# Three bodies behind a branch: the order of expert widths in a two-layer hybrid backbone

## The chip, the core and the metric

The kernel runs on one core of a Trainium2 chip. The metric is the device time of one execution in microseconds (us). TensorE (PE, its sequencer PEq or PEldq), VectorE (DVE), ScalarE (ACT), GpSimd (POOL) and SyncE (SP) each run a stream of instructions of their own and meet through semaphores. All DMAs of weights are issued by SP.

## What is computed

Two layers over 256 latent tokens and 256 context tokens, model width 1024. Both layers mix tokens (gated linear attention and a short convolution). The first layer's channel mixer is a dense SwiGLU, the second's is a mixture of experts over the 256 latent tokens only:

```
def swiglu(h, w1, w3, w2):
    return (jax.nn.silu(h @ w1) * (h @ w3)) @ w2

logits = (h @ w_r).astype(jnp.float32)
vals, idx = lax.top_k(logits, TOP_K)                  # TOP_K = 2 of N_EXPERTS = 8
wts = jax.nn.softmax(vals, axis=-1)
comb = jnp.sum(jax.nn.one_hot(idx, N_EXPERTS) * wts[..., None], axis=-2)
for e in range(N_EXPERTS):
    out = out + comb[..., e:e + 1] * swiglu(h, w1e[e], w3e[e], w2e[e])
```

An expert's three matrices are 1024 x 3584, 1024 x 3584 and 3584 x 1024 in float32. How many tokens choose an expert is known only when the kernel runs: 512 choices over 8 experts, 64 on average.

## The kernel before

Everything up to the router runs without branches. Then each expert `e` is worked through in turn. SP issues its weights without a branch: 42 pieces of 1 MB per expert (`ORDER`, L74), into a ring of 10 slots (`ESLOTS`), 6 pieces for each of the 7 blocks (`NB`) of 512 hidden columns: four of the gate and up matrices (L535), two of the down matrix (L539). A piece may be loaded when the piece ten places ahead of it in the ring's order has been used; `frees` (L478) on PE says so.

PE, ACT and DVE each hold three bodies for each expert, and pick one by its number of tokens:

- `few(e)`: up to 64 tokens (`FEW`). PE multiplies in float32, 64 columns wide (L947 gate and up, L973 down). ACT applies Silu, DVE the product.
- `mid(e)`: 65 to 128 tokens. Each weight piece is split into a rounded part (ACT, L1428) and a remainder (DVE, `low_part`, L1520), and PE makes three products (L1017, L1019, L1024).
- `big(e)`: 129 to 256 tokens, two tiles of float32 products.

The bodies end alike: PE gathers the tokens of expert `e + 1` (L902), turns its weights (L909) and, in `add_slots`, spreads the expert's output over the tokens (L927). DVE adds these sums to the accumulator (L1950). PE may begin `e + 1` only when all four sums are added (`sum_done`), and a middle body also needs its first rounded part from ACT.

The choice is made anew on each of the three engines. Each reads the count of expert `e` from `cnt_i` into a register (L1157 PE, L1471 ACT, L2061 DVE) and calls `by_width`, which writes two nested tests. In the instruction stream the bodies stand one after another: test, `few`, an unconditional jump to the next expert, second test, `mid`, a jump, `big`, a jump. A test that fails jumps to what stands behind the body. The counts are made by PE (L889, L890) and copied to `cnt_i` by DVE (L1906) before `route_ready` lets the experts start.

In the streams of PE the three bodies hold 831, 1186 and 1681 instructions (1 for a wait or branch, 2 for a rounded matmul or a transpose, 4 for a float32 matmul). On ACT they hold about 35, 117 and 46.

With this kernel's inputs experts 0, 1 and 4 take `mid` and the five others `few`.

## Time and profile before

| | before |
|---|---|
| median of 3 runs | 2024.03 us (2020.35 to 2026.72) |
| profiled execution | 2023.0 us |
| its span | 2021.2 us |
| mean granted clock of PE in it | 0.94 of full speed |
| PE busy | 1799.6 us (89%) |
| DVE, ACT busy | 819.5 us (41%), 524.7 us (26%) |
| the experts | from 1038 to about 2000 us of the span |

The times below are of one profiled execution, in us from the span's start, and durations of single instructions in ns. A row of the timeline gives start, duration, engine, line, operation, what it writes and reads, how many, and in brackets how long its engine was idle before it and what ended that; "issue" means that nothing which the profile shows was waited for. Branches, register loads and waits belong to the sequencers (PEldq, ACTq, DVEq) and are not counted as busy; the view of a source line shows them with their durations.

### The profile page before, as it was taken

The page shows a single profiled execution, that of the slowest core. Times are in us where ns is not written, and L with a number is a line of the kernel's source. Part 1 is how long each engine was busy: PE and PEld are TensorE (multiplying, and loading weights), DVE is VectorE, ACT ScalarE, POOL GpSimd, SP SyncE. Part 2 cuts the span into 40 slices and gives each one's busy share as a digit, 9 for nine tenths or more (in the row PEclk, how much of TensorE's full clock was granted, in tenths as well). Part 3 has the DMA queues.
Part 4 walks back from the last instruction along what each step waited for, and adds up shares of the span by engine and source line. Part 5 has one row for each costly group of instructions (what it writes and reads, how often), then busy time and mean ns, then how long its engine had stood idle before and what let it go on. Part 6 is the DMA issues. An engine that isn't in the chain of part 4 may idle for free.

```text
span 2021.2 us, 19505 instructions
## 1 busy us (share of the span) xinstructions
PE 1799.6 (89%) x7958; PEld 1117.3 (55%) x7958; DVE 819.5 (41%) x1146; ACT 524.7 (26%) x656; POOL 2.3 (0%) x12
## 2 busy tenths in 40 slices
PE   5999979999999998997979989898877998887876
PEld 2344435378887875476778768633325883332322
DVE  1044341354443766135269788601105871010102
ACT  3321023330000013212357567400004750000001
POOL 0000000000000000000000000000000000000000
PEclk9899999999999998898879999999998999889998
DMA  9323198523322023222339979799999998999994
GB/s 342 122 83 125 35 365 308 159 91 112 97 84 97 18 76 125 83 84 84 115 137 376 344 263 376 265 359 394 393 396 353 374 346 301 396 391 395 394 394 172
DMA packets 223828, 476.21 MB, mean 236 GB/s; under 512 B 9906, under 2 KB 32724, under 8 KB 223700
## 3 DMA queue, kind: packets, MB, share of 16 engines
q1 hardware_dynamic: 222176, 474.24, 64.0%
q8 instruction: 86, 1.41, 0.3%
q10 hardware_dynamic: 1524, 0.21, 0.1%
q14 instruction: 42, 0.34, 0.0%
HBM read 473.38 MB, written 1.05 MB: 235 GB/s over the span
## 4 chain that ended last, share of the span: by engine, by line
PE 72%; SPq 12%; DMA 7%; issue 3%; DVE 3%; ACT 2%; ACTq 0%; DVEq 0%; POOL 0%; POOLq 0%
PE ps L646 9%; SPq L535 9%; PE ps L652 6%; PE ps L654 6%; PE ps L653 6%; PE ps L1017 6%; PE ps L1019 6%; PE ps L947 6%; PE ps L1024 6%; PE ps L813 4%; DMA ring<-in_e_w 4%; SPq L539 3%; PE ps L704 3%; PE ps L688 3%; PE ps L591 2%
## 5 line engine op out<-in xcount | busy, mean ns | idle before, releaser
L947 PE MATMUL ps<-ring,work 128*64 128x512 f32 x1120 | 286.3, 661 | 85.9 <-DMA ring<-in_e_w 64.4
L947 PEld LDWEIGHTS ps<-ring,work 128*64 128x64 f32 x1120 | 91.6, 151 | 256.7 <-issue 256.7
L1520 DVE TENSOR_TENSOR ring_rounded<-ring,hT_rounded 128x2048 fp32r<-128x2048 f32 x84 | 191.7, 2289 | 28.1 <-ACT hT_rounded L1428 21.7
L1967 DVE TENSOR_TENSOR mixT<-work,ps 64x256 f32<-64x256 f32 x70 | 29.7, 424 | 425.4 <-ACT work L1409 424.3
L646 PE MATMUL ps<-hT,ring 128*128 128x512 f32 (+2 forms) x544 | 182.4, 494 | 0.0
L1428 ACT CAST hT_rounded<-ring 128x2048 fp32r<-128x2048 f32 x84 | 159.9, 1911 | 44.8 <-PE ps L1019 35.0
L646 PEld LDWEIGHTS ps<-hT,ring 128*128 128x128 f32 (+1 forms) x544 | 99.6, 185 | 80.2 <-issue 73.0
L652 PE MATMUL ps<-mixT_rounded,work_rounded 128*128 128x512 f32 x352 | 138.4, 393 | 6.0 <-DVE hT_rounded L1520 5.2
L653 PE MATMUL ps<-hT_rounded,work_rounded 128*128 128x512 f32 x352 | 138.1, 392 | 0.0
L654 PE MATMUL ps<-mixT_rounded,ring_rounded 128*128 128x512 f32 x352 | 137.9, 392 | 0.0
L973 PE MATMUL ps<-ring,mixT 128*64 128x512 f32 x560 | 125.7, 593 | 0.0
L1017 PE MATMUL ps<-hT_rounded,work_rounded 128*128 128x512 f32 x252 | 102.7, 407 | 22.9 <-issue 19.6
L1520 DVE TENSOR_TENSOR ring_rounded<-ring,norms_rounded 128x2048 fp32r<-128x2048 f32 x42 | 96.1, 2289 | 22.8 <-ACT norms_rounded L1428 22.8
L1019 PE MATMUL ps<-hT_rounded,work_rounded 128*128 128x512 f32 x252 | 100.7, 400 | 0.0
L1517 DVE CAST work_rounded<-ring 128x1024 fp32r<-128x1024 f32 (+1 forms) x88 | 49.1, 558 | 123.8 <-PE ps L654 123.8
L1024 PE MATMUL ps<-ring_rounded,work_rounded 128*128 128x512 f32 x336 | 91.4, 394 | 0.0
L1520 DVE TENSOR_TENSOR ring_rounded<-ring,work_rounded 128x1024 fp32r<-128x1024 f32 (+1 forms) x88 | 84.1, 955 | 1.5
L813 PE MATMUL ps<-mixT,ring 128*128 128x512 f32 (+1 forms) x256 | 83.1, 486 | 1.3 <-issue 1.3
L1411 ACT COPY mixT<-ps 128x256 f32<-128x256 f32 x35 | 13.0, 372 | 272.2 <-PE ps L961 272.2
L973 PEld LDWEIGHTS ps<-ring,mixT 128*64 128x64 f32 x560 | 41.0, 137 | 76.7 <-issue 70.2
L1428 ACT CAST norms_rounded<-ring 128x2048 fp32r<-128x2048 f32 x42 | 80.3, 1912 | 9.3 <-issue 6.9
L652 PEld LDWEIGHTS ps<-mixT_rounded,work_rounded 128*128 128x128 f32 x352 | 66.8, 190 | 21.1 <-issue 7.2
(228 smaller groups left out, 2400.1 us busy)
## 6 DMA issues: line engine op xcount, KB each, us to landing
ring<-in_e_w SPq DMA_DIRECT2D x336, 1024.0 KB, 13.7
ring<-in_w_mod SPq DMA_DIRECT2D x24, 2048.0 KB, 16.9
ring<-in_w_in SPq DMA_DIRECT2D x12, 2048.0 KB, 11.1
ring<-in_w SPq DMA_DIRECT2D x22, 1024.0 KB, 7.9
ring<-in_w_out SPq DMA_DIRECT2D x4, 2048.0 KB, 14.1
ring<-in_w SPq DMA_DIRECT2D x4, 2048.0 KB, 7.8
ring<-in_w SPq DMA_DIRECT2D x2, 1536.0 KB, 6.6
mixT<-in_ctx SPq DMA_DIRECT2D x2, 512.0 KB, 4.2
```

The lines of the kernel that those rows point to most:

```text
L535: sp.dma_start(dst.rearrange("p (k n) -> p k n", k=4), rows(w[0, e, k0 * P:(k0 + 4) * P], b * BLK, BLK)).then_inc(piece_in[s], 16)
L646: ins = pe.matmul(acc[0:width, 0:TOK - c0], w[:, k, m * P:m * P + width], hT[:, k, c0:], start=(k == 0), stop=(k == KD - 1))
L652: pe.matmul(acc, w_high_, x_high_, start=first, stop=False)
L653: pe.matmul(acc, w_high_, x_low_, start=False, stop=False)
L654: return pe.matmul(acc, w_low_, x_high_, start=False, stop=last)
L947: ins = pe.matmul(acc[H * w:H * w + H, :], x[:, k, 0:H], piece_words(e, b, 2 * half + w)[:, kk * BLK:(kk + 1) * BLK], start=(k == 0), stop ...
L973: ins = pe.matmul(ps[0][H * half:H * half + H, :], eh[:, b % 2, ((j % 2) * 2 + j // 2) * H:][:, 0:H], piece_words(e, b, 4 + i)[:, o:o + BL ...
L1017: pe.matmul(outs[q], high[q], w_high_[:, cols], start=q < first, stop=False, skip_group_check=True)
L1019: ins = pe.matmul(outs[q], low[q], w_high_[:, cols], start=False, stop=False, skip_group_check=True)
L1024: ins = pe.matmul(outs[q], high[q], w_low_[:, q * BLK:(q + 1) * BLK], start=False, stop=q >= 4 - last, skip_group_check=True)
L1428: act.copy(highs[at_ % HIGHS], piece_words(e, b, i)).then_inc(high_ready, 1)
L1520: return dve.tensor_tensor(dst, src, high, ALU.subtract)
```

## The change

DVE turns the counts into a class before the experts start: 0 for 65 to 128 tokens (`MID`), 1 for more (`BIG`), 2 for up to 64 (`SMALL`). The three engines load the class in place of the count, and `by_width` tests it so that the body for 65 to 128 tokens stands first in each stream, that for more second and the narrow one last. The bodies themselves are the same. The new lines stand some lines further down: L85 becomes L89, L88 L92, L947 L951, L1017 L1021.

```
-def by_width(eng, chosen, few, mid, big):
-
-    with eng.If(chosen < FEW + 1):
-        few()
+
+MID, BIG, SMALL = 0, 1, 2
+
+
+def by_width(eng, width, few, mid, big):
+
+    with eng.If(width < MID + 1):
+        mid()
     with eng.Else():
-        with eng.If(chosen < P + 1):
-            mid()
+        with eng.If(width < BIG + 1):
+            big()
         with eng.Else():
-            big()
+            few()
...
-                chosen = pe.value_load(cnt_i[0:1, e:e + 1], min_val=0, max_val=SEQ)
-                by_width(pe, chosen, lambda: few(e), lambda: mid(e), lambda: big(e))
+                width = pe.value_load(width_i[0:1, e:e + 1], min_val=0, max_val=SMALL)
+                by_width(pe, width, lambda: few(e), lambda: mid(e), lambda: big(e))
...
-            drains(dve.tensor_copy(cnt_i[:], acc[0:1, 2 * NE:3 * NE]), ("pos",))
+            width, chosen = small[0:1, 15, :], acc[0:1, 2 * NE:3 * NE]
+            step(dve.tensor_scalar(width, chosen, FEW + 0.5, float(SMALL), ALU.is_lt, ALU.mult))
             wait_step()
+            drains(dve.scalar_tensor_tensor(out=width, in0=chosen, scalar=P + 0.5, in1=width,
+                                            op0=ALU.is_gt, op1=ALU.add), ("pos",))
             step(dve.tensor_scalar(place, place, 1.0, None, ALU.subtract))
             step(dve.memset(yacc, 0.0))
 
             step(dve.memset(hid, 0.0))
             wait_step()
             wait_drained(dve, ("pos",))
+            step(dve.tensor_copy(width_i[:], width))
+            wait_step()
             dve.tensor_copy(small[:, 14, 2:3], ones[:, 0:1]).then_inc(route_ready, 1)
```

The same two lines change on ACT and on DVE as on PE.

In PE's stream, where the bodies of expert 0 end and those of expert 1 begin, stood before:

```order
L902 MATMUL ps<-work 128x128 x16
L909 MATMUL ps<-ident,work 128x128 x2
L927 MATMUL ps<-work 128x256 x16
L90 UNCONDITIONAL_BRANCH
L1157 TENSOR_LOAD cnt_i
L1157 ISA x2
L85 COMPARE_AND_BRANCH
L947 MATMUL ps<-ring,work 64x512 x24
```

and stands now:

```order
L906 MATMUL ps<-work 128x128 x8
L913 MATMUL ps<-ident,work 128x128 x2
L931 MATMUL ps<-work 128x256 x8
L94 UNCONDITIONAL_BRANCH
L1161 TENSOR_LOAD width_i
L1161 ISA x2
L89 COMPARE_AND_BRANCH
L1021 MATMUL ps<-hT_rounded,work_rounded 128x512
```

The last body of an expert was the wide one (L927 sixteen times) and is the narrow one, and behind the next expert's test stands the middle body (L1021) in place of the narrow one (L947).

In PE's stream, where the first body of expert 0 ends, stood before the end of the narrow body, the jump and the second test, then the middle body:

```order
L961 MATMUL ps<-ident,mixT 128x128 x2
L973 MATMUL ps<-ring,mixT 64x512 x16
L902 MATMUL ps<-work 128x128 x8
L909 MATMUL ps<-ident,work 128x128 x2
L927 MATMUL ps<-work 128x256 x8
L85 UNCONDITIONAL_BRANCH
L88 COMPARE_AND_BRANCH
```

Now the end of the middle body stands there, then the second test and the wide body:

```order
L1023 MATMUL ps<-norms_rounded,mixT_rounded 128x512
L1028 MATMUL ps<-ring_rounded,mixT_rounded 128x512 x4
L906 MATMUL ps<-work 128x128 x8
L913 MATMUL ps<-ident,work 128x128 x2
L931 MATMUL ps<-work 128x256 x8
L89 UNCONDITIONAL_BRANCH
L92 COMPARE_AND_BRANCH
```

In DVE's stream, between the counts and the first selection of tokens, stood before:

```order
L1904 SCALAR_TENSOR_TENSOR small<-ps,small 128x16
L1906 CAST cnt_i<-ps 1x8
L1908 TENSOR_SCALAR small<-small 128x16
L1909 MEMSET work 128x2048
L1911 MEMSET mixT 128x1024
L1914 COPY small<-ones 128x1
L1923 TENSOR_SCALAR work<-work,small 128x256
```

and stands now:

```order
L1908 SCALAR_TENSOR_TENSOR small<-ps,small 128x16
L1911 TENSOR_SCALAR small<-ps 1x8
L1913 SCALAR_TENSOR_TENSOR small<-ps,small 1x8
L1915 TENSOR_SCALAR small<-small 128x16
L1916 MEMSET work 128x2048
L1918 MEMSET mixT 128x1024
L1921 CAST width_i<-small 1x8
L1923 COPY small<-ones 128x1
L1932 TENSOR_SCALAR work<-work,small 128x256
```

The copy of the counts has become two small operations, and a third one writes the classes as integers ahead of the operation that lets the other engines go (L1923).

## Rows read from the trace of the kernel before

**Rows 1.** Timeline of PE: first matmul of experts 0 to 5, first behind the experts.

```profile
1038.06 0.47 PE L1017 MATMUL ps<-hT_rounded,work_rounded 128*128 128x512 f32 x1 [3.25 <-ACT hT_rounded L1428]
...
1175.06 0.77 PE L1017 MATMUL ps<-hT_rounded,work_rounded 128*128 128x512 f32 x1 [7.63 <-issue]
...
1310.39 1.12 PE L947 MATMUL ps<-ring,work 128*64 128x512 f32 x2 [5.72 <-issue]
...
1421.45 1.12 PE L947 MATMUL ps<-ring,work 128*64 128x512 f32 x2 [3.48 <-issue]
...
1539.96 0.76 PE L1017 MATMUL ps<-hT_rounded,work_rounded 128*128 128x512 f32 x1 [11.99 <-issue]
...
1673.31 0.65 PE L947 MATMUL ps<-ring,work 128*64 128x512 f32 x2 [3.58 <-issue]
...
2001.91 0.77 PE L591 MATMUL ps<-norms,ones 128*128 128x256 f32 x1 [2.82 <-ACT norms L1203]
```

**Rows 2.** Lines L85, L88, by stretch: count, ns min/median/max, first to last start.

```profile
L85 PEldq COMPARE_BRANCH  x1: 3865/3865/3865, 1033.5 to 1033.5; - x1
...
L88 PEldq COMPARE_BRANCH  x1: 3270/3270/3270, 1166.3 to 1166.3; - x1
...
L85 PEldq COMPARE_BRANCH  x1: 4122/4122/4122, 1170.3 to 1170.3; - x1
...
L88 PEldq COMPARE_BRANCH  x1: 3702/3702/3702, 1303.5 to 1303.5; - x1
...
L85 PEldq COMPARE_BRANCH  x1: 88/88/88, 1308.0 to 1308.0; - x1
...
L85 PEldq COMPARE_BRANCH  x2: 77/3127/6177, 1413.8 to 1420.7; - x2
...
L85 PEldq COMPARE_BRANCH  x2: 6266/6610/6954, 1525.5 to 1532.5; - x2
...
L88 PEldq COMPARE_BRANCH  x1: 3340/3340/3340, 1668.6 to 1668.6; - x1
...
L85 PEldq COMPARE_BRANCH  x2: 77/3186/6296, 1775.7 to 1782.7; - x2
...
L85 PEldq COMPARE_BRANCH  x2: 77/3150/6222, 1887.5 to 1894.4; - x2
...
L85 PEldq COMPARE_BRANCH  x1: 4944/4944/4944, 1996.3 to 1996.3; - x1
```

**Rows 3.** Stretches: length, busy time by engine, PE clock, DMA share, GB/s.

```profile
1305.00:1308.00 3.00, 0.00 (x0) 0.00 (x0) 1.15 (x3) 0.00 (x0) 0.00 (x0) 1.00 0.03 8
1419.00:1422.00 3.00, 0.55 (x2) 0.32 (x4) 0.29 (x1) 0.00 (x0) 0.00 (x0) 0.50 1.06 388
```

**Rows 4.** Page: the instruction queue; the narrow body's first products, five experts.

```profile
q8 instruction: 86, 1.41, 0.3%
...
L947 PE MATMUL ps<-ring,work 128*64 128x512 f32 x1120 | 286.3, 661 | 85.9 <-DMA ring<-in_e_w 64.4
```

**Rows 5.** Issue to landing, L535: all issues, then those at 1426.8, 1788.6, 1900.8.

```profile
DMA to landing us min/median/max: 5.0/12.4/20.2
...
DMA to landing us min/median/max: 8.1/8.1/8.1
...
DMA to landing us min/median/max: 8.3/8.3/8.3
...
DMA to landing us min/median/max: 9.4/9.4/9.4
```

**Rows 6.** Timeline of DVE and ACT: end of expert 3, and the copied counts.

```profile
1527.03 1.88 DVE L1950 TENSOR_TENSOR work<-work,ps 128x512 f32<-128x512 f32 x3 [0.17 <-PE ps L927]
...
1527.36 1.90 ACT L1428 CAST hT_rounded<-ring 128x2048 fp32r<-128x2048 f32 x1 [4.53 <-issue]
...
1024.41 0.14 DVE L1906 CAST cnt_i<-ps 1x8 int32<-1x8 f32 x1
```

More of the change, by code:

```diff
@@ L254, in hybrid_backbone @@
         small = sb("small", [P, 16, NE])
-        cnt_i = sb("cnt_i", [1, NE], I32)
+        width_i = sb("width_i", [1, NE], I32)
         eps = sb("eps", [P, 1])
@@ L1470, in _ @@
             for e in range(NE):
-                chosen = act.value_load(cnt_i[0:1, e:e + 1], min_val=0, max_val=SEQ)
-                by_width(act, chosen, lambda: few(e), lambda: mid(e), lambda: big(e))
+                width = act.value_load(width_i[0:1, e:e + 1], min_val=0, max_val=SMALL)
+                by_width(act, width, lambda: few(e), lambda: mid(e), lambda: big(e))
             act.wait_ge(sum_done, 4 * NE)
@@ L2060, in _ @@
             for e in range(NE):
-                chosen = dve.value_load(cnt_i[0:1, e:e + 1], min_val=0, max_val=SEQ)
-                by_width(dve, chosen, lambda: few(e), lambda: mid(e), lambda: big(e))
+                width = dve.value_load(width_i[0:1, e:e + 1], min_val=0, max_val=SMALL)
+                by_width(dve, width, lambda: few(e), lambda: mid(e), lambda: big(e))
             add_experts(modv[:, 1, 5])
```

## The prediction

> **What bounds the kernel now.** I read first when TensorE starts each expert, then the branches themselves, then the DMA queue. PE's first matmul of each expert stands in [rows 1]: experts 0, 1 and 4 run the body for 65 to 128 tokens (their first matmul is L1017), experts 2, 3, 5, 6 and 7 the narrow one (L947). In every row but the first and the last, what the profile puts before the start is "issue", idle time of 3.5 to 12 us in which the engine waited for nothing that another engine does. [Rows 2] say what it was: the branch instructions on PE's sequencer. A branch that is not taken costs 77 to 88 ns. Every taken one, of either kind, costs microseconds: 3.27, 3.70 and 3.34 (end of the middle body), 3.87 and 4.12 (the jump past the narrow body) where the weight transfers stand still, 6.18, 6.27, 6.30 and 6.22 (end of the narrow body) and 6.95 (the jump past it, before expert 4) where they run, and 4.94 at the very end. [Rows 3] show the two conditions: from 1305 us the ring of weight pieces is full and DMA moves 8 GB/s, from 1419 us it moves 388. The instructions themselves come by DMA, in packets of 1.41 MB / 86 = 16.4 KB ([rows 4]), so a target far away must first be brought in, behind the weights.
>
> What a PE delay costs depends on the body. In the middle body PE is the bound: expert 4 takes 1673.31 - 1539.96 = 133.4 us with its pause ([rows 1]), 3.2 us for each of its 42 pieces of 1.05 MB, and DMA at 388 GB/s needs 2.7. So a delay before experts 0, 1 and 4 counts in full. The narrow body is bound by DMA, and there the issue of the eleventh piece decides, since it waits for the first piece that PE frees. An issue needs at least 5.0 us to land. At experts 3, 6 and 7 that piece landed 8.1, 8.3 and 9.4 us after its issue ([rows 5]): it stood behind others, and could have been issued 3.1, 3.3 and 4.4 us later at no cost. At experts 2 and 5, which follow a middle body, the queue is dry ([rows 3]) and there is no such reserve: PE's delay is the queue's delay, and every later piece inherits it.
>
> **The change part by part.** PE, ACT and DVE get the same new order. I count PE's taken branches between two experts:
> - middle to middle: two before, one now
> - narrow to middle: two before, none now (the narrow body stands last and runs into the next expert's load)
> - middle to narrow: one before, three now (past two bodies; past the middle one; past the one for over 128)
> - narrow to narrow: one before, two now.
>
> *Saved.* Before expert 1 the jump of 4.12 us falls away; PE needs then what follows a branch, about 0.6 us: 4.2 us gained. Before expert 4 both jumps go, 6.27 and 6.95 us, but PE may not start before DVE has added expert 3's sums, which ends at 1527.03 + 1.88 = 1528.9 ([rows 6]). ACT's first cast, now at 1527.36 behind 4.53 us of issue, moves ahead of that with its own jumps. So PE starts near 1529.1 in place of 1539.96: 10.9 us gained. Expert 4 then runs with a ring that is less full, but DMA's advantage over the expert, 42 x (3.2 - 2.7) = 21 us, refills it before expert 5 takes its eleventh piece. Together -15.1 us.
>
> *Added, middle to narrow.* The test of the class follows the end of a jump by 0.7 us (1525.5 + 6.27 = 1531.8, then 1532.5). So before expert 5 it came at 1668.6 + 3.34 + 0.7 = 1672.7, and PE started 0.6 us later, at 1673.31. Now that test is a jump, in the same place as the one of 4.12 us, and a second one right behind it. No row shows two with nothing between. Its bounds are the cheapest single jump, 3.3 us, and the one of 4.94 us; I take 4.1, the row where a jump followed a landing most closely without traffic. 4.1 + 4.1 - 0.1 = 8.1 us, all on the path. Before expert 2 the same, less 1.7: there the test ended at 1308.1 and PE began only at 1310.39, 2.3 us later in place of 0.6, and I take this for a packet end close behind the landing (7 instructions, below), which the new landing does not have: 6.4 us. Together 14.5.
>
> *Added, narrow to narrow.* The first jump, with traffic, replaces the one that went (6.2 us either way); the second is new: between 6.2 and 7.8 (6.95 plus the 0.8 by which 4.94 exceeds 4.12), taken at 6.95. PE starts 6.9 us later at experts 3, 6 and 7. Less the reserves 3.1 and 3.3: 3.8 and 3.6 us lost. Expert 7 has one thing more. Counted in the built program (a float32 matmul as two loads and two matmuls) the bodies have 831, 1186 and 1681 instructions. If a packet holds 256 of them, the stop of 1.7 us before expert 2 puts a packet's end 7 instructions behind that landing, at 16068 of PE's stream; 83 packets on, at 37316, lies another, and the changed kernel lands for expert 7's narrow body at 37312, 4 instructions before it. The next packet then has to be waited for: 0 to 6.2 us, a whole fetch in traffic. I take 5.2, since the fetch may be ordered at the landing and about 1 us passes before the fifth instruction. The other landings have 88 instructions or more ahead. So 6.9 + 5.2 - 4.4 = 7.7 us. Together 15.1.
>
> *Nothing or nearly.* DVE's routing gains two operations of about 0.15 us (as L1906, [rows 6]) and one wait on the path ahead of the first gather: +0.4. Before expert 0 PE's jump of 3.87 us goes, but its first matmul waited for ACT's cast ([rows 1]), where only the short jump of ACT goes: -0.4. The jumps that ACT and DVE gain before narrow bodies (4.5 us each by [rows 6], two or three in a row) are covered by PE's own jumps and its first block of matmuls, 286.3 / 35 = 8.2 us ([rows 4]), which both wait for; without that cover the last 4.5 us would stand on the path. At the end PE's 4.94 us go too, but L591 waits for ACT's squares ([rows 1]): 0.
>
> **Sum:** -15.1 + 14.5 + 15.1 + 0 = +14.5 us. On the profiled execution, 2023.0 us (1.8 beyond its span of 2021.2), that is 2037.5. The median of the runs shown lies 1.0 above it; I add half: 2038.
>
> **A rule against the rows.** The untaken branches cost 77 to 88 ns and the taken ones 3.27 us and more ([rows 2]). The Trainium skill ("Advanced Engine Details and Errata", Control Flow Timing) gives about 51 ns for a branch that is always taken and about 108 ns for compare-and-branch. By this the order of the bodies would be worth nothing that can be measured; it fits the untaken branches and not the taken ones.
>
> **The rivals.**
> - *Faster: the second of two adjacent jumps is nearly free.* If the sequencer resolves the second branch before it orders the first target's packet, a pair costs what one costs. For it: ACT and DVE get over short distances without a stop. Against it: the pair before expert 4 cost 6.27 and 6.95, not less. It gives -15.1 + 2.3 + 4.0 + 0 + 0 + 0.8 = -8, so 2015. It decides where a second jump costs below about 2.2 us without and 3.2 us with traffic: there the sum crosses zero. The Trainium skill ("Runtime: NRT & Kernel Launch", Instruction fetch mechanics) gives TensorE an instruction memory of 2048 instructions; by this, targets past 1186 or 1681 could be held already. The jump of 6.95 us went past 831, which speaks against it.
> - *Mild: each second jump at its lower bound, no packet end at expert 7.* 3.3 and 6.2 us: -15.1 + 12.9 + 3.1 + 2.9 + 1.8 = +5.6, so 2029.
> - *Harsh: upper bounds.* 4.9 and 7.8 us: -15.1 + 16.1 + 4.7 + 4.5 + 8.6 = +19; and TensorE, at 0.50 of its clock in the window from 1419 us ([rows 3]), may begin narrow bodies slow for longer: up to 2047.
> - *No effect.* The durations in [rows 2] would be a wait for something that meets PE wherever two bodies meet, whatever stands between, and with branches of 0.1 us the sum is the +0.4 of the routing: 2023.4. Against it: one price with traffic, another without, and none where a branch is not taken.
>
> **How the numbers follow.** Forecast 0.60 (2032 to 2042), harsh 0.12, mild 0.14, no effect 0.05, second jump free 0.09. About 0.3%, 6 us, is what a measurement of this kernel can tell from no change. Faster 0.09; same 0.14 + 0.05 = 0.19; slower 0.72. The range takes in the forecast, the mild case and the harsh one, 2026 to 2047, and leaves out the other two.
>
> **What would show it.** In the changed profile, branch rows on PE: pairs of 4 and 4 us before experts 2 and 5, of 6 and 7 before 3, 6 and 7, and under 0.1 us before 1 and 4. PE's start of expert 4 within 1.5 us of DVE's last L1950. The eleventh piece of experts 3, 6 and 7 landing near 5 us after its issue, since the queue has run dry. Five microseconds between the last branch and the first matmul of expert 7. I am wrong if pairs cost as much as one jump, if the reserve of [rows 5] is larger than landing times tell, or if expert 4 starves because its ring starts less full.

## The result, and the profile after

| | before | after |
|---|---|---|
| median | 2023.85 us (2020.35 to 2026.72) | 2051.95 us (2046.72 to 2052.58) |
| ratio of the runs | | 1.0137, 95% interval 1.0125 to 1.0149 |
| span of the profiled execution | 2021.2 us | 2050.8 us |
| mean granted clock of PE | 0.941 | 0.928 |

The kernel became slower by 28.1 us, where 14 were foretold: the sign was right and the size was half. The measured time lies above the range.

The timeline of PE in the changed kernel shows the first matmul of each expert, the second group of expert 7, and the first matmul behind the experts (start, duration, line, and in brackets the idle time ahead and what ended it). It answers to [rows 1].

```profile
1041.86 0.76 PE L1021 MATMUL ps<-hT_rounded,work_rounded 128*128 128x512 f32 x1 [2.89 <-ACT hT_rounded L1432]
...
1174.90 0.76 PE L1021 MATMUL ps<-hT_rounded,work_rounded 128*128 128x512 f32 x1 [3.89 <-issue]
...
1317.32 1.12 PE L951 MATMUL ps<-ring,work 128*64 128x512 f32 x2 [13.21 <-issue]
...
1435.34 1.12 PE L951 MATMUL ps<-ring,work 128*64 128x512 f32 x2 [10.63 <-issue]
...
1545.16 0.77 PE L1021 MATMUL ps<-hT_rounded,work_rounded 128*128 128x512 f32 x1 [0.98 <-DVE work L1959]
...
1687.63 1.12 PE L951 MATMUL ps<-ring,work 128*64 128x512 f32 x2 [12.39 <-issue]
...
1806.82 1.12 PE L951 MATMUL ps<-ring,work 128*64 128x512 f32 x2 [10.98 <-issue]
...
1925.71 1.94 PE L951 MATMUL ps<-ring,work 128*64 128x512 f32 x2 [11.57 <-issue]
...
1928.72 1.12 PE L951 MATMUL ps<-ring,work 128*64 128x512 f32 x2 [1.07 <-issue]
...
2031.41 1.19 PE L595 MATMUL ps<-norms,ones 128*128 128x256 f32 x2 [2.82 <-ACT norms L1207]
```

Set against the starts before (1038.06, 1175.06, 1310.39, 1421.45, 1539.96, 1673.31, 1783.37, 1895.11, 2001.91), each start less the one before it gives what every expert gained or lost:

| from | to | change, us | PE's jumps there |
|---|---|---|---|
| start | expert 0's first matmul | +3.8 | one fewer |
| 0 | 1 | -4.0 | one fewer |
| 1 | 2 | +7.1 | two more |
| 2 | 3 | +7.0 | one more |
| 3 | 4 | -8.7 | two fewer |
| 4 | 5 | +9.1 | two more |
| 5 | 6 | +9.1 | one more |
| 6 | 7 | +7.2 | one more |
| 7 | end | -1.1 | one fewer |

Of the first 3.8 us, 2.4 stood there before the router's counts were made: the profiled execution after is simply later by that much in a part that the change doesn't touch. Another 0.3 is DVE's new work ahead of the first gather. Most of the rest is the gather itself, 32 products that both kernels have, before and after:

```profile
1029.41 5.17 PE L902 MATMUL ps<-work 128*128 128x128 f32 x32 [5.13 <-DVE work L1925]
```

```profile
1032.10 6.66 PE L906 MATMUL ps<-work 128*128 128x128 f32 x32 [5.44 <-DVE work L1934]
```

Before, the granted clock was 0.50 from 1025.4 to 1032.3 us, after from 1027.8 to 1038.1: the whole gather ran at the lower level (1.2 GHz).

The branches on PE's sequencer, by line and stretch (count, ns, start), answer to [rows 2]:

```profile
L89 PEldq COMPARE_BRANCH  x1: 4344/4344/4344, 1307.3 to 1307.3; - x1
L92 PEldq COMPARE_BRANCH  x1: 5022/5022/5022, 1311.7 to 1311.7; - x1
...
L89 PEldq COMPARE_BRANCH  x1: 6306/6306/6306, 1420.8 to 1420.8; - x1
L92 PEldq COMPARE_BRANCH  x1: 7534/7534/7534, 1427.2 to 1427.2; - x1
...
L89 PEldq COMPARE_BRANCH  x1: 82/82/82, 1540.3 to 1540.3; - x1
...
L89 PEldq COMPARE_BRANCH  x1: 4142/4142/4142, 1678.1 to 1678.1; - x1
L92 PEldq COMPARE_BRANCH  x1: 4719/4719/4719, 1682.3 to 1682.3; - x1
...
L92 PEldq COMPARE_BRANCH  x1: 7562/7562/7562, 1917.6 to 1917.6; - x1
```

The pairs stand where they were foretold. The first of a pair costs about what the single jump in its place cost, 4.1 to 4.3 us without traffic and 6.2 to 6.3 with it. The second, right behind it, costs 4.7 to 5.0 and 7.5 to 7.6: dearer than the values taken (4.1 and 6.95), inside the bounds.

Now the weight queue. The eleventh piece of expert 3 is issued at 1441.7 us, and the view of its line (L539 now, L535 before) gives:

```profile
L539 SPq DMA_DIRECT2D ring<-in_e_w x1: 368/368/368, 1441.7 to 1441.7; - x1
...
DMA to landing us min/median/max: 5.2/5.2/5.2
```

In [rows 5] it took 8.1: the queue has run dry, as foretold, at experts 6 and 7 too (5.2 us each). The windows of expert 3's start show more than that. First before, then after (length, busy time of PE, PEld, DVE, ACT, POOL, granted clock of PE, DMA share, GB/s):

```profile
1413.00:1423.00 10.00, 6.14 (x20) 3.97 (x22) 3.70 (x7) 0.00 (x0) 0.00 (x0) 0.58 1.05 386
1423.00:1433.00 10.00, 10.00 (x44) 3.45 (x42) 0.85 (x2) 0.59 (x1) 0.00 (x0) 0.91 1.04 397
```

```profile
1412.00:1420.00 8.00, 4.94 (x31) 2.90 (x28) 2.32 (x4) 1.65 (x3) 0.00 (x0) 1.00 1.05 384
1420.00:1440.00 20.00, 9.37 (x28) 5.04 (x28) 3.03 (x6) 0.00 (x0) 0.00 (x0) 0.51 0.89 331
1440.00:1448.00 8.00, 8.00 (x38) 2.72 (x34) 0.85 (x2) 0.59 (x1) 0.00 (x0) 0.95 0.63 206
```

Before, PE is at the lower level for about 10 us around the jump. After, it stays there for 20: the second jump's idle 7.5 us, and then the first products. These products free the first piece, so the eleventh piece is issued 6.4 us after PE's start instead of 5.3.

### The profile page after: what moved, and what is told of

The parts are those of the page before. It is cut to its first block, busy times and chain, and to the rows that moved or that the text cites. A ratio compares the mean times of both kernels' runs of the same rounds, so it can differ in the third digit from the quotient of the medians.

```text
span 2050.8 us, 19498 instructions
## 1 busy us (share of the span) xinstructions
PE 1812.9 (88%) x7958; PEld 1123.4 (55%) x7958; DVE 819.9 (40%) x1148; ACT 524.6 (26%) x656; POOL 2.3 (0%) x12
## 3 DMA queue, kind: packets, MB, share of 16 engines
HBM read 473.38 MB, written 1.05 MB: 231 GB/s over the span
## 4 chain that ended last, share of the span: by engine, by line
PE 73%; SPq 11%; DMA 6%; issue 4%; DVE 3%; ACT 2%; ACTq 0%; DVEq 0%; POOL 0%; POOLq 0%
PE ps L650 9%; SPq L539 8%; PE ps L656 6%; PE ps L658 6%; PE ps L951 6%; PE ps L657 6%; PE ps L1021 6%; PE ps L1023 6%; PE ps L1028 5%; PE ps L817 4%; DMA ring<-in_e_w 4%; PE ps L708 3%; SPq L543 3%; PE ps L692 3%; PE ps L595 3%
## 5 line engine op out<-in xcount | busy, mean ns | idle before, releaser
L951 PE MATMUL ps<-ring,work 128*64 128x512 f32 x1120 | 292.0, 669 | 117.4 <-issue 59.9
L951 PEld LDWEIGHTS ps<-ring,work 128*64 128x64 f32 x1120 | 93.4, 153 | 291.7 <-issue 291.7
L1524 DVE TENSOR_TENSOR ring_rounded<-ring,hT_rounded 128x2048 fp32r<-128x2048 f32 x84 | 191.7, 2289 | 13.2 <-ACT hT_rounded L1432 11.8
L1021 PE MATMUL ps<-hT_rounded,work_rounded 128*128 128x512 f32 x252 | 103.1, 409 | 7.8 <-issue 3.9
L1413 ACT ACTIVATE work<-ps 64x512 f32<-64x512 f32 x35 | 20.6, 589 | 244.7 <-PE ps L951 244.7
## 6 DMA issues: line engine op xcount, KB each, us to landing
ring<-in_w_out SPq DMA_DIRECT2D x4, 2048.0 KB, 13.9
```

Source lines behind the costliest of these rows:

```text
L951: ins = pe.matmul(acc[H * w:H * w + H, :], x[:, k, 0:H], piece_words(e, b, 2 * half + w)[:, kk * BLK:(kk + 1) * BLK], start=(k == 0), stop ...
L1021: pe.matmul(outs[q], high[q], w_high_[:, cols], start=q < first, stop=False, skip_group_check=True)
L1524: return dve.tensor_tensor(dst, src, high, ALU.subtract)
```

## The ledger

From the traces of both kernels, for the three narrow-to-narrow places, in us: the later start of PE (beyond the shift of the last piece of the expert before), the longer first block up to the issue of the eleventh piece, the part that the piece's wait in the queue absorbed, and what was lost further on until the expert's last piece.

| expert | PE starts later by | first block | absorbed | further on | sum | forecast |
|---|---|---|---|---|---|---|
| 3 | 7.4 | +1.1 | -2.9 | +2.0 | +7.6 | 6.9 - 3.1 = 3.8 |
| 6 | 7.8 | +1.4 | -3.1 | +1.3 | +7.5 | 6.9 - 3.3 = 3.6 |
| 7 | 7.5 | +1.9 | -4.2 | +1.3 | +6.5 | 6.9 + 5.2 - 4.4 = 7.7 |

The column of sums is the shift of the expert's last piece. The stop of 1.07 us stands in the first block of expert 7. For delays of this size the reserve was read rightly (2.9, 3.1, 4.2 against 3.1, 3.3, 4.4). What was missing are a slower first block and a loss after the queue starts again: within eight pieces behind the dry stretch one piece lands about 1.2 us late, in this kernel and, at experts 2 and 5, in the kernel before as well.

The traces say which piece that is. At expert 6 the 18th piece landed 3.86 us after the 17th, where the others follow each other by 2.6 to 2.7, and the windows from 1831.9 to 1834.6 and from 1834.6 to 1838.5 us, the transfers of the 17th and the 18th, hold:

```profile
q1 hardware_dynamic: 528, 1.05, 105.6%
```

```profile
q1 hardware_dynamic: 747, 1.50, 103.2%
q8 instruction: 1, 0.02, 1.8%
```

One packet of PE's instructions (queue 8) began in the second. The sixteen traces here hold 80 narrow bodies. In 54 the queue was dry, or within 2 us of it, when the eleventh piece was issued, and each has a late piece: in 47 the one during whose transfer PE's first packet of instructions begins, between the 13th and the 26th, in 5 the eleventh itself, again with such a packet, and in 2 the one next to it. In the 26 others PE's packets make no piece late. (At expert 3 after, two are late, the 12th by 1.1 us and the 26th by 0.5.) No experiment was made for this, so the link is read from the traces alone, and why a packet costs something only then is open.

## Experiments

The ratios are to the kernel before on the same chip, with 95% intervals.

### One part of the change alone

PE with the new order, ACT and DVE with the narrow body first (`few_first`):

```
+def few_first(eng, width, few, mid, big):
+    with eng.If(width > BIG):
+        few()
+    with eng.Else():
+        with eng.If(width < MID + 1):
+            mid()
+        with eng.Else():
+            big()
...
-                by_width(act, width, lambda: few(e), lambda: mid(e), lambda: big(e))
+                few_first(act, width, lambda: few(e), lambda: mid(e), lambda: big(e))
...
-                by_width(dve, width, lambda: few(e), lambda: mid(e), lambda: big(e))
+                few_first(dve, width, lambda: few(e), lambda: mid(e), lambda: big(e))
```

> PE alone has the new order of bodies; ACT and DVE keep the narrow body first. Theory A (PE's taken branches are what costs, ACT's and DVE's are covered): as the changed kernel, +25 to +30 us on before, with pairs of 4.3 and 5 us before experts 2 and 5 and of 6.3 and 7.5 before 3, 6 and 7. Before expert 4 ACT's first cast keeps its 4.5 us of issue and DVE its 5.1, so PE may wait for the first remainder: up to 3 us more. Rival B (ACT or DVE carry a good part, since every block passes through them): +15 us or less.

Measured 2056.31 us, 1.0174 (1.0157 to 1.0191), 34 us and so above the 25 to 30 expected. PE's order alone does the harm, and a little more: expert 4, which takes 5.9 us longer than in the changed kernel, now waits for DVE once its own jumps are gone. PE's timeline at expert 4's first product with a remainder:

```profile
1549.40 0.79 PE L1039 MATMUL ps<-ring_rounded,work_rounded 128*128 128x512 f32 x1 [3.67 <-DVE ring_rounded L1535]
```

The other way round, `few_first` on PE and the new order on ACT and DVE:

```
-                by_width(pe, width, lambda: few(e), lambda: mid(e), lambda: big(e))
+                few_first(pe, width, lambda: few(e), lambda: mid(e), lambda: big(e))
```

> ACT and DVE have the new order, PE keeps the narrow body first. Theory A: 0 to +1 us on before, since PE's own jumps are as before and only the routing of the classes is added. Rival B: +10 us or more.

Measured 2026.26 us, 1.0012 (1.0000 to 1.0025): their jumps are covered by PE's, as the prediction had it.

The classes alone, with `few_first` on all three engines:

> Only the classes worked out by DVE, with the old order on all three engines. Theory A: +0.3 to +1 us on before. Rival C (the computing and loading of a class is what costs, the order little): +15 us or more.

Measured 2024.13 us, 1.0011 (1.0002 to 1.0021), 0.4 to 4 us by the interval: the classes themselves are cheap.

### Where the gains and the losses are

The classes, with the middle body first for experts 1 and 4 only (`mid_first`: middle, then narrow, then wide) and `few_first` for the others:

```
-                by_width(pe, width, lambda: few(e), lambda: mid(e), lambda: big(e))
+                (mid_first if e in (1, 4) else few_first)(pe, width, lambda: few(e), lambda: mid(e), lambda: big(e))
```

and so on ACT and DVE.

> Classes as in the change, narrow body first for all experts but 1 and 4, where the middle body stands first and the wide one last. So a jump falls away before experts 1 and 4 and none is added anywhere. Theory A, from the rows: 4.1 us gained before expert 1, 6.9 before expert 4 (its start near 1533 in place of 1540), 0.5 lost for the classes: -10.5 us, between -8 and -12. Rival C: slower by what the classes cost. Rival D (expert 4's lead is eaten by its emptier ring): -5 or less.

Measured 2014.59 us, 0.9956 (0.9939 to 0.9974): expert 1 started 2.9 us earlier and expert 4 another 5.9, less than the 4.1 and 6.9 expected; up to 0.7 us was added at each of the others. The jumps themselves gave back all that was expected (4.1 and 7.1 us from the first jump to the first product). What is missing stands ahead of them, where the clock was low. Expert 0 took 129.5 us up to its jump in place of 128.2, with a granted clock of 0.50 for 6.8 us around its start in place of 3.4. Expert 3's last sums, 2.96 us long before (shown further below), took 4.44:

```profile
1524.18 4.44 PE L953 MATMUL ps<-work 64*128 64x256 f32 x16 [3.06 <-DVE work L2005]
```

The change holds a gain, once it is confined to the experts that take this body.

The kernel before with the narrow body last and reached by one jump in place of two, without classes (the middle and the wide body stand within the outer test):

```
-    with eng.If(chosen < FEW + 1):
-        few()
-    with eng.Else():
+    with eng.If(chosen > FEW):
...
+    with eng.Else():
+        few()
```

> No classes; the counts are tested as before, but the outer test asks for more than 64 tokens and holds the middle and the wide body, and the narrow body is its other branch, last in the stream. A narrow body then costs one jump past both others instead of two, the middle one none. Taken jumps on PE: middle to middle 1, narrow to middle 0, middle to narrow 2, narrow to narrow 1 (before: 2, 2, 1, 1). Theory A (each taken jump on PE has its price, the second of a pair the highest): about 4.2 us gained before expert 1, 8.9 before expert 4; 4.3 added before experts 2 and 5 each, less the 1.7 us stop before expert 2; nothing before 3, 6 and 7, where a jump in replaces a jump out: -6 us, between -9 and -3. Rival E (what costs is that the narrow body stands last, far from the load, not the number of jumps): slower than before by 10 us or more.

Measured 2019.63 us, 0.9983 (0.9974 to 0.9992). Experts 1 and 4 began 3.5 and 9.2 us earlier, 2 and 5, with one jump more than before, 2.1 and 5.5 later. Narrow to narrow has one jump as before, and experts 3, 6 and 7 changed by -0.7, +0.3 and -0.1 us. So it is the number of jumps that counts, not the order of the bodies. The gain stayed at the small end of the range, since 1.9 us were lost behind the start of expert 7, where PE stopped after two products:

```profile
1889.81 1.94 PE L947 MATMUL ps<-ring,work 128*64 128x512 f32 x2 [3.18 <-issue]
1895.22 1.12 PE L947 MATMUL ps<-ring,work 128*64 128x512 f32 x2 [3.47 <-issue]
```

The next packet of instructions began at 1892.7 us, 3.5 after the landing, with weights moving. This is a stop of the kind that the prediction had expected at expert 7 of the changed kernel.

### A second jump right behind a first

The changed kernel with 24 idle instructions (3.6 us) between the two tests on PE:

```
     with eng.Else():
+        if between is not None:
+            for _ in range(24):
+                eng.sem_inc(between, 1)
         with eng.If(width < BIG + 1):
```

> The changed kernel with 24 idle sequencer instructions (3.6 us) on PE between the first and the second test. Theory G (the second jump costs 5.0 and 7.5 us because it is ordered right behind a landing, together with the packet that follows the landing): the second jump falls to 3.3 to 4.3 us before experts 2 and 5, and to 6.2 to 7.0 before 3, 6 and 7. Rival H (its price comes from what it jumps over or from its place): it stays at 4.7 to 5.0 and 7.5. The kernel as a whole is slower than the changed one by 8 to 16 us either way.

Measured 2059.33 us, 1.0178 (1.0159 to 1.0198). Those are 8 us more than the changed kernel, by the ratios. The second jumps, five of them, by line:

```profile
L95 PEldq COMPARE_BRANCH  x5: 3757/6057/6277, 1312.7 to 1927.0; - x5
```

They fell to 3.8 and 3.9 us without traffic and 6.1 to 6.3 with it, from 4.7 to 5.0 and 7.5 to 7.6. The instruction queue shows what adjacency changes. In the changed kernel, the second jump before expert 7 runs from 1917.6 us, and the windows 1914.9 to 1916.1 (the first jump's fetch) and 1920.8 to 1921.6 (the second's) hold, in packets, MB and share:

```profile
q8 instruction: 1, 0.02, 5.5%
...
q8 instruction: 2, 0.03, 28.1%
```

For one jump one packet comes. For the second, two come together. I read them as the one that follows the first landing in the stream, which no jump asked for, and the target; the record of a packet does not say which it is. In the spaced kernel each second jump has one packet of its own again. No packet of PE's queue (q8) moves between 1917.6 and 1920.8. In the trace of the packets, the two took 1.37 and 2.22 us, one alone about 1.05. The packet after a jump starts 3.7 us after the jump where weights are moving and about 1 us after it where they are not. The difference of 2.7 us is as long as one weight piece takes at 388 GB/s; that the packet stands behind just one piece is a reading, not shown.

### What a delay of PE costs without any jump

The kernel before with idle instructions ahead of the narrow bodies of experts 3, 6 and 7, 20 of them (3.0 us) and 48 (7.2 us):

```
+                if e in (3, 6, 7):
+                    for _ in range(20):
+                        pe.sem_inc(idle, 1)
```

> The kernel before, with 20 idle sequencer instructions on PE (about 0.15 us each, 3 us together) ahead of the narrow bodies of experts 3, 6 and 7: a delay of PE with no jump in it. Theory R (the eleventh piece has a reserve of 3.1, 3.3 and 4.4 us): 0 to +2 us. Rival F (no reserve, the DMA queue inherits every delay): +9 us.

Measured 2029.89 us, 1.0028 (1.0017 to 1.0040), more than the 0 to 2 us of a full reserve. Until their last piece the three experts lost 1.7, 4.5 and 0.6 us. Expert 6 began 5.1 us later in place of 3.0, since the next packet of instructions had not come when the idle ones were through (below). At expert 3 the eleventh piece was issued 2.8 us late, inside the reserve of 3.1, and yet landed 1.7 us late, 7.0 us after its issue. At expert 7 the reserve held: of a delay of 3.3 us, 0.6 was lost, which leaves rival F out. Why expert 3 differs is open.

> The same with 48 such instructions, 7.2 us. Theory R as in the prediction, delay less reserve: 4.1 + 3.9 + 2.8 = +10.8 us. Theory R2 (as R, and each time the queue has run dry it loses 1.2 to 1.8 us more in the pieces after it, and PE's first block at half clock takes 1.1 to 1.4 us longer): +17 to +20. Rival F: +21.6 and more, with the same steps already at the delay of 3 us.

Measured 2041.63 us, 1.0093 (1.0077 to 1.0108): 18.8 us, in the range of R2 and far from R's 10.8, with no jump added. The three experts lost about 7.2, 7.1 and 5.5 us until their last piece. The jumps thus cost about what any idle time of PE costs there, and the reserve of 3 to 4 us is largely eaten by what follows the delay: a slower first block and the restart of the queue.

The same delay with TensorE at work, to take the clock out: eight products in place of the idle instructions.

```
+                if e in (3, 6, 7):
+                    for _ in range(8):
+                        pe.matmul(ps[2][0:H, :], x[:, 0, 0:H], x[:, 0:4, :], start=True, stop=True,
+                                  skip_group_check=True)
```

> The kernel before with eight extra products (64x512, float32, into a sum that the body's first product overwrites; they add work and change nothing that is kept) at the start of the narrow bodies of experts 3, 6 and 7. They hold PE for about 5 x 1.12 + 3 x 0.56 = 7.3 us, as long as the 48 idle instructions (7.2 us) did, but with TensorE at work. If part of the loss after a delay is the slower clock of the body's first block, the granted clock is back at full before the eleventh piece is issued, and the steps at experts 3, 6 and 7 fall from 7.8, 7.9 and 7.0 us with idle instructions to 5.5 to 6.5, the run from +18.8 us to +13 to +16 (ratio 1.0065 to 1.0080). If the loss is the queue's alone (delay less about 3 us of reserve, and more where the ring runs dry), it stays at 1.009.

Measured 2040.81 us, 1.0097 (1.0075 to 1.0118). The windows of expert 3's start, with idle instructions and then with products:

```profile
1421.00:1429.00 8.00, 0.58 (x2) 0.32 (x4) 0.00 (x0) 0.00 (x0) 0.00 (x0) 0.50 1.03 393
1429.00:1433.00 4.00, 4.00 (x12) 1.32 (x10) 0.00 (x0) 0.00 (x0) 0.00 (x0) 0.50 0.18 73
```

```profile
1418.00:1426.00 8.00, 7.82 (x16) 2.44 (x18) 0.00 (x0) 0.00 (x0) 0.00 (x0) 0.78 1.04 397
1426.00:1430.00 4.00, 4.00 (x21) 1.57 (x20) 0.00 (x0) 0.00 (x0) 0.00 (x0) 1.00 0.28 114
```

The total did not fall, against the first expectation. But the experiment was not clean: the products held PE for 7.7, 8.9 and 8.2 us, not 7.2, the second with a wait for a packet of instructions. The body's first block ran at full clock in 4.5 us (6.5, 6.1 and 6.5 with idle instructions). From the untaken test to the issue of the eleventh piece 12.7, 13.9 and 13.2 us passed, 1.8, 0.3 and 1.4 less than with idle instructions; the experts lost 5.6, 6.8 and 5.5 us against 7.2, 7.1 and 5.5. So the slower clock is part of the loss, through the first block: at experts 3 and 6 what the issue gained (1.8 and 0.3), the expert gained (1.5 and 0.3). Most of the loss is the queue's. At expert 7 the 1.4 us gave nothing back: a packet of PE's instructions began 0.6 us after the eleventh piece was issued, and the piece took 7.2 us to land, where 5.1 is usual on a dry queue.

### Ends of packets

The kernel before with ten idle instructions ahead of the first gather, which move every later landing against the packets' ends:

```
+            for _ in range(10):
+                pe.sem_inc(idle, 1)
             gather(0, 0)
```

> The kernel before, with ten idle one-count semaphore increments on PE's stream ahead of the first gather, so that every later instruction of PE moves ten places against the ends of the 256-instruction packets. Nothing else changes; ten of them cost about 1 us where PE waits anyway. Packet-end theory (a landing that lies a few instructions ahead of a packet's end stops a second time for the next packet): the landing before expert 2 moves from 7 instructions ahead of an end to 254, so PE's first matmul there follows its untaken test by 0.6 us in place of 2.3, and experts 2 and 3 start 1.7 us earlier; in all -1.5 to -2 us. Rival (the 2.3 us is a fixed cost of that place, or waits for something else): expert 2 starts as before, ratio 1.000.

Measured 2022.73 us, 0.9996 (0.9980 to 1.0013): over the whole run nothing. At the place itself the expected happened:

```profile
L85 PEldq COMPARE_BRANCH  x1: 88/88/88, 1310.6 to 1310.6; - x1
...
1311.30 1.56 PE L948 MATMUL ps<-ring,work 128*64 128x512 f32 x4 [3.54 <-issue]
```

From the untaken test to the first matmul 0.6 us pass, 2.3 in [rows 1, 2], and expert 2 took 2.2 us less to begin. But expert 0 began 1.4 us later, and expert 1 another 1.7. The trace has the cause: the first gather took 6.64 us in place of 5.17, and expert 0's body 129.5 up to its jump in place of 128.2, both with the granted clock at 0.50 for 3.4 us longer; the other 0.5 is in the jumps of that place. The first gather takes 6.5 to 6.7 us in all nine traces with either the classes or these ten instructions ahead of it, and 5.2 to 5.3 in the seven with neither.

The changed kernel with the same ten:

> The changed kernel with the same ten idle instructions. Its narrow landing for expert 7 moves from 4 instructions ahead of a packet's end to 251. By the term of the prediction (a whole fetch in traffic waits there) 5.2 us come back against the changed kernel; by the changed kernel's trace, where only one stop of about 1 us stands some instructions behind the landing, 1 to 1.5 us: ratio to the kernel before 1.0131 against 1.0137, and the 1.07 us stop at the start of expert 7 gone. Rival: the stop stays, since it has another cause.

Measured 2044.86 us, 1.0116 (1.0086 to 1.0147). The interval holds both expectations, so the place must decide. The stop of 1.07 us at expert 7 is gone, its first block takes 6.0 us in place of 7.6, and from the last piece of expert 6 to its own last piece expert 7 gets 5.1 us later in place of 6.5: 1.4, the size that the trace gave, not the 5.2 of the prediction. (Its profiled execution is 4 us shorter up to the first expert, which this edit doesn't explain.)

This trace also shows the clock's part with the jumps as they are. At expert 6 the granted clock was back at full 3.3 us into the first block, in the changed kernel 6.1. PE began 7.6 us late (7.8 there), but the first block was not longer than before, and the expert lost 6.0 us in place of 7.5.

The kernel before, with the outer test `chosen > FEW` and the middle body first for experts 1 and 4, its own order for the others, and the ten idle instructions:

```
+def mid_first(eng, chosen, few, mid, big):
+    with eng.If(chosen > FEW):
+        with eng.If(chosen < P + 1):
+            mid()
+        with eng.Else():
+            big()
+    with eng.Else():
+        few()
```

> The kernel before with its counts (no classes) and its order of bodies, except that for experts 1 and 4 the test for more than 64 tokens stands outside and the middle body first; ten idle instructions as in the padded kernel before. From the runs so far: before expert 1 one jump of 4.1 us goes (-3 to -4), before expert 4 two go (-6 as measured with this placement, -9 as measured in the changed kernel), expert 2 and 5 gain nothing beyond the packet end (-1.7): -10 to -14 us, 2010 to 2014. Rival: the order for expert 4 gives its gain back at expert 5, whose narrow body now stands behind two others: -6, 2018.

Measured 2017.02 us, 0.9982 (0.9967 to 0.9996), the rival's number, but not by the rival's reason. Expert 4 began 6.9 us earlier and took 4.4 longer. Its sixth product was held up:

```profile
1527.56 0.79 PE L1031 MATMUL ps<-hT_rounded,work_rounded 128*128 128x512 f32 x1 [2.17 <-issue]
```

The jump out of expert 3 had landed at 1521.6 us, with a packet's end some 16 to 20 instructions ahead; PE went on 6.0 us after the landing, 1.6 after the next packet had come. So pads that cure one landing can spoil another, and these ten, ahead of the gather, make expert 0 start 1.9 us later, counted from the router's counts, than in the next kernel, which has none there. In the next kernel they stand where they cost nothing, in wide bodies that these inputs never run:

```
+                for _ in range({0: 10, 2: 24, 5: 12}.get(e, 0)):
+                    pe.sem_inc(idle, 1)
```

> As the kernel of counts with the middle body first for experts 1 and 4, but without the ten idle instructions ahead of the experts. In their place 10, 24 and 12 idle instructions stand in the wide bodies of experts 0, 2 and 5, which are never run with these inputs, so they cost nothing and only move packet ends: the landings for experts 2 and 6 lie 253 instructions ahead of an end, the middle body of expert 4 starts 242 ahead of one (16 in the kernel before this one, whose expert 4 stopped 2.17 us after its second product). Packet-end theory: that stop goes and expert 4 takes 133 to 134 us, not 137.7; -3.5 at expert 1, -1.7 at expert 2, -7 to -9 at expert 4, nothing given back at expert 5: -12 to -14 us, 2010 to 2012, ratio 0.993 to 0.994. Rival (expert 4 loses because its ring starts less full or its clock stays low whatever the packets do): 2016 to 2018, as before.

Measured 2012.05 us, 0.9953 (0.9937 to 0.9968). Expert 4 took 133.3 us, as expected. But expert 6 began 5.75 us late. The load of its count, by line and start:

```profile
L1171 PEldq TENSOR_LOAD <-cnt_i x1: 308/308/308, 1764.5 to 1764.5; - x1
L1171 PEldq FUSED_REGOPS  x1: 152/152/152, 1770.5 to 1770.5; - x1
```

The first instruction behind the landing ran at 1764.5, the second at 1770.5. Between them, at 1767.8, one packet of instructions began. A packet ended one instruction behind the landing; by my count it should have ended three instructions before it, so the count was four off by then. The last run moves that landing by eight instructions (20 in place of 12):

> As the kernel before it, with 20 idle instructions in place of 12 in the wide body of expert 5 (never run). In that kernel the first instruction behind the landing for expert 6 ran at 1764.5 us and the second only at 1770.5: a packet's end lay one instruction behind the landing, and the next packet took a whole fetch in traffic, 5.8 us, which the expert lost (step +5.75 us). Eight instructions further on, the landing lies behind that end and has 245 or more ahead of it. Packet-end theory: the stop is gone, expert 6 is 5.7 us shorter than in that kernel, in all -15 us, about 2007, ratio 0.992 to 0.993. Rival (the stop belongs to the place or to that one execution, not to the count of instructions): it stays, ratio 0.995.

Measured 2008.29 us, 0.9929 (0.9906 to 0.9952), 14.5 us faster than the kernel before. Its interval meets that of the last kernel, so the step between the two is shown by the place and not by the totals. Expert 6 began 5.5 us earlier relative to expert 5 than in the last kernel, without a stop:

```profile
1773.04 1.98 PE L959 MATMUL ps<-ring,work 128*64 128x512 f32 x4 [3.04 <-issue]
```

This beats both kernels. It is made for which experts take which body with these inputs; others would be computed as well, but not as fast.

## Why the prediction was right in sign and half in size

The step that failed is the narrow-to-narrow term, "PE starts 6.9 us later, less the reserve". It gave 15.1 us, of which 5.2 were for a packet's end at expert 7; the runs showed 21.6, of which about 1.1 for that stop. The rest of the term was thus 9.9 against 20.5. The second jump was mis-sized (6.95 us taken, 7.5 measured), and two losses stood at nothing without a reason: a longer first block, and the lateness behind a queue that has run dry. That the packet's end was dear in the forecast hid 4 us of this: without it the sum would have been 9.3.

- **Jumps as the bound:** right. Only taken branches cost, and pairs stood where they were foretold. The rivals of a free second jump and of no effect are out. The Trainium skill ("Runtime: NRT & Kernel Launch", Instruction fetch mechanics) says that a taken branch whose target is outside the current two-page window forces a DMA fetch before execution goes on. The packets of the trace agree; I had weighed the size of the instruction memory and passed over that sentence.
- **Saved, expert 1:** -4.2 forecast, -4.0 measured.
- **Saved, expert 4:** -10.9 forecast, -8.7 measured. PE started 0.3 us after DVE's last addition, as the prediction had it, but that came late. The sixteen products of expert 3's last sums, before and after:

```profile
1525.00 2.96 PE L927 MATMUL ps<-work 64*128 64x256 f32 x16 [3.06 <-DVE work L1974]
```

```profile
1539.16 5.03 PE L931 MATMUL ps<-work 64*128 64x256 f32 x16 [3.06 <-DVE work L1983]
```

```profile
1540.00:1544.00 4.00, 4.00 (x14) 2.99 (x12) 1.97 (x3) 2.42 (x2) 0.00 (x0) 0.50 1.05 388
```

  The third fence is the window of the same stretch after: the granted clock is 0.50 (1.2 GHz). The prediction took the time of DVE's last sum over from the trace of before; it stands behind 2.1 us more of PE. Expert 4 did not starve: 129.0 us from its first product to its jump, 128.6 before.
- **Added, middle to narrow:** expert 2 +6.4 forecast, +7.1 measured; expert 5 +8.1 forecast, +9.1 at its start, and 10.4 with the slower first block and the restart of the queue. The term mis-sized is the second adjacent jump (4.1 taken; 5.0 and 4.7).
- **Added, narrow to narrow:** +15.1 forecast, 7.6 + 7.5 + 6.5 = 21.6 measured. Mis-sized were the second jump (6.95 taken; 7.5) and, more, two things set at nothing: the first block at the lower clock (+1.1, +1.4 and, without the stop, +0.8) and the loss after a dry queue (+2.0, +1.3 and +1.3). The reserve itself was right here, where the delay was larger than it; at expert 3 of the kernel with 20 idle instructions a smaller delay was not absorbed whole. The harsh rival had named jump and clock, and put the clock into its bound only in passing.
- **Packet's end at expert 7:** 5.2 forecast, about 1.1 measured. The mechanism is right, as the stops of 3.5 us at expert 7 in the kernel with one jump and of 5.6 at expert 6 in the last experiments show; the place and the state of the queue were not. I had four instructions between landing and end; two float32 products (eight instructions) passed before the stop, the same four off as in the last experiments, and the next packet began at 1926.4, 1.3 us after the landing, since the queue was dry by then.
- **Nothing or nearly:** the routing cost 0.3 (forecast 0.4). Expert 0 began 1.1 us later still, where 0.4 less was forecast; its branch fell from 3.87 us to 0.09, yet it waits for ACT's cast as before. The runs with classes in which PE keeps the old order show the same 1.1 and 1.5, so that is not the work of the new order: it is the gather at the lower clock, 1.5 us longer, less the 0.4. A delay of 0.3 us was enough to leave it there. The end: -0.1 beyond the queue's shift.

Forecast 14.5; measured 29.5 at the end of the experts in the profiled execution, of which 2.4 lie ahead of the change. The 12.6 between them: 4.7 from the queue's restarts, 4.4 from first blocks (the stop of 1.1 among it) and 2.0 from late sums, 2.0 from second jumps in traffic, 2.5 at experts 2 and 5, 1.4 up to expert 0, less 5.2 for the packet's end; the rest is the reserves (0.6), expert 1 (0.2) and rounding.

## What to carry over

Count taken branches on the engine that bounds the kernel, and treat each as a fetch by DMA that queues behind the data: 3.3 to 3.9 us on an idle queue here and 6.1 to 6.4 behind weights, 4.7 to 5.2 and 7.5 to 7.7 for the second of a pair. Put first the body that each place needs, not one body for all places; one that only falls through pays nothing. When a delay is set against a reserve in a queue, add what comes after the delay: the clock that fell while the engine idled, and a restart of the queue.

## What was not expected of the hardware

- A packet's end right behind a landing costs up to a whole fetch: 5.6 us with traffic (one instruction behind), 3.5 (about eight behind), 2.2 (16 to 20 behind), 1.7 without traffic. Padding in a body that is never run moves it at no cost.
- After a jump the next packet in order begins about 0.8 us behind the landing, without traffic, though no jump asked for it (at 1307.3 us in the changed kernel, landing at 1306.5). A jump taken 0.7 us after a landing costs 4.0 to 4.8 us without traffic in place of 3.3 to 3.9.
- A piece of 1 MB issued to a dry queue mostly lands after 4.9 to 5.5 us. Of the six that took longer (5.7 to 7.2), five had a packet of PE's instructions begin during their transfer.
- After a dry restart of the queue one piece lands about 1.2 us late, nearly always the one into whose transfer PE's first packet of instructions falls (52 of 54). Where the queue had not run dry such packets made no piece late (26 of 26). Why is open.
- A delay of 0.3 us ahead of the first gather, by the classes or by ten idle instructions on PE, went with a granted clock of 0.50 through its whole length: 6.5 to 6.7 us in place of 5.2 to 5.3.
